# Streaming encoder step: the bias table's product in another PSUM bank and copied by ScalarE, and two more weight units in the second pair of split buffers

## The chip, the core and the metric

The kernel is one program on one core of one Trainium2 chip. The metric is the time that one execution takes on the device, in microseconds (us), as the median of several executions. The engines are TensorE (PE in the profile; PEld is its loading of weights), VectorE (DVE), ScalarE (ACT), GpSimd (POOL) and SyncE (SP, which here only issues DMAs). They run side by side and wait for each other by semaphores.

## What is computed

One inference step of a hybrid encoder layer, for a prompt of 512 tokens and 8 x 16 sample tokens, 640 tokens in all. Cut to what matters here:

```python
h = rms_norm(x, p['norm1_g'])
proj = h @ p['w_in']                                   # 1024 x 4424, all in float32
q, k, v, qi, ki, wi, p_rw, ga, gb = split_cols(proj, IN_SPLITS)
att = dsa_attention(q, qi, wi, k_all, v_all, ki_all, q_pos, k_pos, rel_bias)
rw, wkv_T = rwkv7_mix(p_rw, shift0, wkv0, p)
mixed = sigmoid(ga) * (att @ w_att_out) + sigmoid(gb) * (rw @ w_rw_out)
x = x + mixed @ p['w_out']
x = x + square(relu(rms_norm(x) @ w_ff1)) @ w_ff2
# in dsa_attention:
bias = rel_bias[t5_bucket(sel_pos - qp)]               # 32 buckets x 8 heads, by relative position
```

## The kernel before

**Layout and products.** Activations lie by channel, 128 partitions by 8 groups (`KD`) of 640 tokens (`T`). Each float32 product is made of three products of float32r halves: high by high, low by high, high by low. So every weight and every activation is split into a high and a low part. Weights stream in as units of 128 x 512 (`UNIT`): SP loads unit u into `w_raw` (4 slots), GpSimd's `split` (lines 665 to 676) writes the high part (two instructions, lines 672 and 673) and the low part (line 675), and TensorE multiplies. `w_split` counts units that are split, `w_used` units that TensorE is done with.

**The first tiles.** The input projection has 25 tiles of 128 columns (`WIN_TILES`), two units each. Tiles 0 to 3 are multiplied in pairs by `first_tiles` (lines 805 to 829): tiles 0 and 1 into the two halves of the PSUM tensor `acc`, tiles 2 and 3 into `wk_lo` and `wk_hi`, the halves of the other PSUM tensor `wk`. They run on x times g1, since the norm is not known yet. Their units are 0 to 7, of which four at a time lie split: `w_hi`/`w_lo` and, lower in the scratch area, `w_hi_2`/`w_lo_2`, two slots each. From unit 8 on only `w_hi`/`w_lo` are used, so the split of unit u waits until TensorE has used unit u - 2. Tile n from 4 on is `gemm(2 * n, ...)` and `gemm(2 * n + 1, ...)`, lines 898 to 904. Tile 5 (`TILE_K`, units 10 and 11) holds the keys.

**Around the norm.** ScalarE makes the high parts of x times g1 (`x_high`, line 1477) and the squares (`x_square`, line 1483). VectorE makes the low parts (`x_rest`, line 2011) and adds the squares (`x_add`, line 2019). TensorE's `x_stat` (lines 801 and 802) gives the mean square. VectorE then makes the reciprocal root (`newton`), scales x with it (line 2035), and once more low parts are made, of the normed x (`rest_again`, line 2040). Tile 4 is the first that uses the normed x, and waits for its low parts one group at a time (`each=(h_low, ...)`).

**The bias table.** TensorE multiplies the 32 x 8 bias table with a one-hot matrix, 8 x 768 out (lines 793 and 794), into `acc`, bank half 1, where tile 1 goes. VectorE copies it negated into `line` (line 2006) before all its other work; TensorE waits for that copy (`line_ready`) before tile 1. The table is stored to DRAM from tile 5 on.

**What sets the order.** Each engine's order is written out by hand, one block per engine. GpSimd, VectorE and ScalarE each run their instructions strictly in order.

Of the kernel before, what the change touches and what calls it, by code (L numbers as in the profile page):

```python
# [309 lines left out]
def build(nc, dram):  # L310
# [130 lines left out]
    with ExitStack() as ctx:  # L441
# [220 lines left out]
        def _(pool):  # L662
# [15 lines left out]
            def split_units(lo, hi):  # L678

                u = lo  # L680
                while u < hi and (u % RAW or u < RAW or hi - u < 2 * RAW):
                    split(u, 16 * (u // RAW + 1), u - SPLIT + 1 if u >= SPLIT else None, u + 1)
                    u += 1
                if u < hi:
                    with pool.Fori(u // RAW, hi // RAW) as i:
                        for r in range(RAW):
                            split(r, i * 16 + 16, i * RAW + (r - SPLIT + 1), i * RAW + (r + 1))
                    for u in range(hi // RAW * RAW, hi):
                        split(u, 16 * (u // RAW + 1), u - SPLIT + 1, u + 1)

            for u in range(PAIR):
                split(u, 16 * (u // RAW + 1), u - RAW + 1 if u >= RAW else None, u + 1,
                      *((w_hi_2, w_lo_2) if u % RAW >= SPLIT else (w_hi, w_lo)))
            for u in range(PAIR, PAIR + SPLIT):
                split(u, 16 * (u // RAW + 1), u - RAW + 1, u + 1)
            split_units(PAIR + SPLIT, U_GATE + 2)

            pool.wait_ge(masks_in, 16)
            def norm_y(i):
# [72 lines left out]
        def _(pe):  # L772
            mm, tr = nc.tensor.matmul, nc.tensor.transpose

            def gemm(u, out, first, last, x_hi, x_lo, k0, slot=None, each=None):

                pe.wait_ge(w_split, u + 1)
                s = u % SPLIT if slot is None else slot
                for b in range(4):
                    if each is not None:  # L780
                        sems, base_ = each
                        pe.wait_ge(sems[b % len(sems)], base_ + b // len(sems) + 1)
                    w_h, w_l = w_hi[:, s, b * P:(b + 1) * P], w_lo[:, s, b * P:(b + 1) * P]
                    for n, (w_, x_) in enumerate(((w_h, x_hi), (w_h, x_lo), (w_l, x_hi))):
                        go, end = first and b == 0 and n == 0, last and b == 3 and n == 2
                        mm(out[:, 0:CUT], w_, x_[:, k0 + b, 0:CUT], start=go, stop=end)  # L786
                        done = mm(out[:, CUT:T], w_, x_[:, k0 + b, CUT:T], start=go, stop=end)  # L787
                done.then_inc(w_used, 1)
# [1 line left out]


            pe.wait_ge(table_in, 16 * N_TABLE)
            mm(acc[0:NH, 1, A0:A0 + CUT], rb[:], onehot[:, 0:CUT], start=True, stop=True)
            mm(acc[0:NH, 1, A0 + CUT:A0 + LINE], rb[:], onehot[:, CUT:LINE], start=True, stop=True).then_inc(line_mm, 1)


            def x_stat():
# [6 lines left out]
            def first_tiles(n):  # L804

                outs = (wk_lo, wk_hi) if n else tile_acc
                for k0 in range(0, KD, 2):
                    half = k0 // 4
                    his, los = (w_hi, w_hi_2)[half], (w_lo, w_lo_2)[half]
                    for t in range(2):  # L810
                        if k0 % 4 == 0:
                            pe.wait_ge(w_split, RAW * n + 2 * half + t + 1)
                        if n == 0 and k0 == 0 and t == 1:
                            pe.wait_ge(line_ready, 1)
                        if n and k0 == 0 and t == 0:
                            pe.wait_ge(rms_read, 1)
                        for k in (k0, k0 + 1):
                            if n == 0 and t == 0:
                                pe.wait_ge(h_low[k % 2], k // 2 + 1)
                            b = k % 4  # L820
                            w_h, w_l = his[:, t, b * P:(b + 1) * P], los[:, t, b * P:(b + 1) * P]
                            for m, (w_, x_) in enumerate(((w_h, h_hi), (w_h, h_lo), (w_l, h_hi))):
                                go, end = k == 0 and m == 0, k == KD - 1 and m == 2
                                for cols in COLUMNS:
                                    done = mm(outs[t][:, cols], w_, x_[:, k, cols], start=go, stop=end)  # L825
                        if k0 % 4 == 2:
                            done.then_inc(w_used, 1)
                    if n == 0 and k0 == 4:
                        x_stat()
# [68 lines left out]
            first_tiles(1)  # L898
            for n in range(4, WIN_TILES):
                pe.wait_ge(*freed(n - 2 if n >= 6 else n - 4))  # L900
                gemm(2 * n, tile_acc[n % 2], True, False, h_hi, h_lo, 0, each=(h_low, KD // 2) if n == 4 else None)
                score_units(*SCORE_GAPS.get((n, 0), (0, 0)))
                sample_steps(*SAMPLE_GAPS.get((n, 0), (0, 0)))
                gemm(2 * n + 1, tile_acc[n % 2], False, True, h_hi, h_lo, 4, each=(h_low, KD // 2 + 2) if n == 4 else None)
                if phase(n - 1)[1] == 2 and 1 <= phase(n - 1)[0] <= 4:
                    bonus_sums(phase(n - 1)[0] - 1)
                score_units(*SCORE_GAPS.get((n, 1), (0, 0)))
                sample_steps(*SAMPLE_GAPS.get((n, 1), (0, 0)))
                if n == 4:
                    pe.wait_ge(const_in, 16 * N_CONST)  # L910

                    pe.wait_ge(*freed(2))
                    pe.wait_ge(h_full, KD + 2)
                    for t in range(NT):
                        done = tr(wk[:, 0, t * NH:(t + 1) * NH], wit[HD:HD + NH, t * P:(t + 1) * P], ident[HD:HD + NH, HD:HD + NH])
                    done.then_inc(wi_turned, 1)
                j, step = phase(n)
                if step == 0 and 1 <= j <= 4:
                    key_squares(j - 1)
                if step == 1 and 0 <= j <= 3:  # L920
                    codes(j)
# [544 lines left out]
        def _(act):  # L1466
# [12 lines left out]
            def x_square(k):  # L1479

                if k >= 3:
                    act.wait_ge(sum_set, k - 2)
                do(A((wk_lo, wk_hi)[k % 2][:, 0:T] if k else sq[:, 0, :], xT[:, k, :], ACT.Square), sq_ready)

            act.wait_ge(vec_in, 16)
            for i in range(4):
                act.wait_ge(x_in[i], 16)
                if i < 3:
                    x_high(2 * i)
                    x_high(2 * i + 1)  # L1490
                x_square(2 * i)
                x_square(2 * i + 1)
            x_high(6)
            x_high(7)
            act.wait_ge(sq_used, 1)
# [489 lines left out]
        def _(dve):  # L1985
# [15 lines left out]
                do.settle()  # L2001
                do(V.scalar_tensor_tensor(rs, tmp, 1.5, rs, ALU.add, ALU.mult), signal)


            dve.wait_ge(line_mm, 1)
            do(V.tensor_scalar(line[:], acc[0:NH, 1, A0:A0 + LINE], -1.0, None, ALU.mult), line_ready)

            def x_rest(k):

# [636 lines left out]
```

## Time and profile before

| | us |
|---|---|
| median of 3 executions | 1149.45 |
| lowest and highest | 1149.07, 1151.77 |
| the profiled execution | 1146.9 |
| its span | 1144.9 |
| TensorE busy in it | 1100.8 (96%) |
| VectorE busy | 695.0 (61%) |
| GpSimd busy | 630.1 (55%) |
| ScalarE busy | 398.1 (35%) |

The span runs from the first to the last instruction of the profiled execution; its own time is 2.0 us longer. All places below are in us from the start of the span. In a row of the timeline or of the groups, `L2006` is line 2006 of the kernel, `x2` means that two instructions are merged into one row, and the brackets say how long the engine sat idle before the row and what ended that. A matmul of 384 columns and its partner of 256 columns appear as separate rows or as one row of two.

### The profile page before, as it was taken

The page shows a single profiled execution, that of the slowest core. Times are in us where ns is not written, and L with a number is a line of the kernel's source. Part 1 is how long each engine was busy: PE and PEld are TensorE (multiplying, and loading weights), DVE is VectorE, ACT ScalarE, POOL GpSimd, SP SyncE. Part 2 cuts the span into 40 slices and gives each one's busy share as a digit, 9 for nine tenths or more (in the row PEclk, how much of TensorE's full clock was granted, in tenths as well). Part 3 has the DMA queues.
Part 4 walks back from the last instruction along what each step waited for, and adds up shares of the span by engine and source line. Part 5 has one row for each costly group of instructions (what it writes and reads, how often), then busy time and mean ns, then how long its engine had stood idle before and what let it go on. Part 6 is the DMA issues. An engine that isn't in the chain of part 4 may idle for free.

```text
span 1144.9 us, 25256 instructions
## 1 busy us (share of the span) xinstructions
PE 1100.8 (96%) x10421; PEld 1038.1 (91%) x10421; DVE 695.0 (61%) x1173; ACT 398.1 (35%) x757; POOL 630.1 (55%) x687
## 2 busy tenths in 40 slices
PE   7999999989999999999999999999999999999996
PEld 6878989879888889887899999999999999999995
DVE  6863776773555388765344434676358547745777
ACT  4443334443333343333341122343134223413453
POOL 5742456651322047533236655678568857866783
PEclk9999999999999999999999999999999999999998
DMA  7343533220100232222232223222323133113122
GB/s 248 84 88 66 84 91 88 65 90 4 40 3 3 86 101 61 64 76 74 67 136 74 74 74 102 82 74 74 93 73 92 49 100 91 58 56 110 55 75 92
DMA packets 48342, 89.37 MB, mean 78 GB/s; under 512 B 6728, under 2 KB 11216, under 8 KB 48048
## 3 DMA queue, kind: packets, MB, share of 16 engines
q1 hardware_dynamic: 43568, 77.88, 22.6%
q10 hardware_dynamic: 4672, 10.04, 4.3%
q8 instruction: 76, 1.25, 0.5%
q14 instruction: 26, 0.21, 0.1%
HBM read 80.06 MB, written 7.83 MB: 77 GB/s over the span
## 4 chain that ended last, share of the span: by engine, by line
PE 70%; DVE 20%; issue 4%; ACT 4%; POOL 1%; DMA 0%; ACTq 0%; DVEq 0%; POOLq 0%
PE acc L786 17%; PE acc L787 11%; PE wk L1424 8%; PE acc L1424 7%; PE wk L786 6%; PE wk L787 4%; PE wk L940 2%; PE acc L1020 2%; DVE hid_lo L2435 1%; PE acc L1000 1%; PE acc L1022 1%; DVE invs L2228 1%; PE acc L825 1%; PE wk L1306 1%; DVE xT L2035 1%
## 5 line engine op out<-in xcount | busy, mean ns | idle before, releaser
L675 POOL TENSOR_TENSOR w_lo<-w_raw,w_hi 128x512 fp32r<-128x512 f32 x178 | 243.2, 1366 | 14.8
L672 POOL TENSOR_TENSOR w_hi<-w_raw,ones_w 128x32 fp32r<-128x32 f32 x178 | 60.0, 337 | 323.4 <-PE acc L787 260.8
L786 PE MATMUL acc<-h_hi,w_hi 128*128 128x384 f32 x424 | 150.5, 355 | 6.9 <-POOL w_lo L675 4.3
L786 PE MATMUL acc<-h_lo,w_hi 128*128 128x384 f32 x424 | 143.7, 339 | 0.0
L786 PE MATMUL acc<-h_hi,w_lo 128*128 128x384 f32 x424 | 143.7, 339 | 0.0
L673 POOL TENSOR_SCALAR w_hi<-w_raw 128x480 fp32r<-128x480 f32 x178 | 119.7, 672 | 0.0
L787 PE MATMUL acc<-h_lo,w_hi 128*128 128x256 f32 x424 | 118.7, 280 | 0.0
L787 PE MATMUL acc<-h_hi,w_hi 128*128 128x256 f32 x424 | 118.7, 280 | 0.0
L787 PE MATMUL acc<-h_hi,w_lo 128*128 128x256 f32 x424 | 118.6, 280 | 0.0
L786 PEld LDWEIGHTS acc<-h_hi,w_hi 128*128 128x128 f32 x424 | 79.9, 188 | 15.6 <-issue 9.5
L750 POOL TENSOR_TENSOR p_lo<-w_sum,p_hi 128x512 fp32r<-128x512 f32 x44 | 64.9, 1477 | 29.3 <-ACT p_hi L1942 29.3
L787 PEld LDWEIGHTS acc<-h_hi,w_hi 128*128 128x128 f32 x424 | 80.1, 189 | 0.3
L787 PEld LDWEIGHTS acc<-h_lo,w_hi 128*128 128x128 f32 x424 | 80.0, 189 | 0.0
L787 PEld LDWEIGHTS acc<-h_hi,w_lo 128*128 128x128 f32 x424 | 79.9, 189 | 0.0
L786 PEld LDWEIGHTS acc<-h_hi,w_lo 128*128 128x128 f32 x424 | 79.9, 188 | 0.0
L786 PEld LDWEIGHTS acc<-h_lo,w_hi 128*128 128x128 f32 x424 | 79.9, 188 | 0.0
L1911 ACT ACTIVATE squares<-scaled 128x640 f32<-128x640 f32 x32 | 23.7, 741 | 128.6 <-DVE scaled L2442 128.6
L722 POOL TENSOR_TENSOR merge<-br,e_masks 128x512 f32<-128x512 f32 x19 | 24.8, 1316 | 60.8 <-PE acc L1000 30.7
L2228 DVE TENSOR_TENSOR invs<-invs,acc 128x512 f32<-128x512 f32 (+1 forms) x38 | 25.5, 672 | 47.7 <-PE acc L1022 47.4
L2492 DVE TENSOR_TENSOR x<-x,wk 128x320 f32<-128x320 f32 x64 | 30.1, 483 | 26.6 <-PE wk L1424 26.1
L1424 PE MATMUL wk<-hid_hi,p_hi 128*128 128x320 f32 x144 | 44.8, 311 | 1.4 <-DVE scaled L2442 1.3
L2492 DVE TENSOR_TENSOR x<-x,acc 128x320 f32<-128x320 f32 x64 | 30.1, 482 | 26.1 <-PE acc L1424 25.7
(453 smaller groups left out, 3237.8 us busy)
## 6 DMA issues: line engine op xcount, KB each, us to landing
w_raw<-w SPq DMA_DIRECT2D x178, 256.0 KB, 2.6
w_block<-w SPq DMA_DIRECT2D x64, 256.0 KB, 3.0
line_scratch<-line ACTq DMA_DIRECT2D x8, 384.0 KB
xT<-xT SPq DMA_DIRECT2D x4, 640.0 KB, 6.8
x<-xT ACTq DMA_DIRECT2D x1, 2560.0 KB, 9.8
bias_p<-line_scratch SPq DMA_DIRECT2D x8, 256.0 KB, 4.5
kc<-k_cache SPq DMA_DIRECT2D x8, 256.0 KB, 2.6
vc<-v_cache SPq DMA_DIRECT2D x8, 256.0 KB, 2.7
```

The costliest lines, as they stand in the source:

```text
L672: nc.gpsimd.tensor_tensor(hi[:, s, 0:LEAD], w_raw[:, r, 0:LEAD], ones_w[:], ALU.mult).then_inc(w_high, 1)
L673: nc.gpsimd.tensor_scalar(hi[:, s, LEAD:], w_raw[:, r, LEAD:], 1.0, 1.0, ALU.mult, ALU.mult).then_inc(w_high, 1)
L675: nc.gpsimd.tensor_tensor(lo[:, s, :], w_raw[:, r, :], hi[:, s, :].bitcast(F32), ALU.subtract).then_inc(w_split, 1)
L722: nc.gpsimd.tensor_tensor(merge[n % 2][:], br[i % 2][:, :, 0, :], over_heads(m, NH), ALU.mult).then_inc(merge_set, 1)
L750: nc.gpsimd.tensor_tensor(lo, factor(FACTORS[k % PRODUCTS][0]), hi.bitcast(F32), ALU.subtract).then_inc(p_split, 1)
L786: mm(out[:, 0:CUT], w_, x_[:, k0 + b, 0:CUT], start=go, stop=end)
L787: done = mm(out[:, CUT:T], w_, x_[:, k0 + b, CUT:T], start=go, stop=end)
L940: return mm(out, lhsT, rhs, start=start, stop=True, skip_group_check=True)
L1424: done = mm(out, w_[:, b * P:(b + 1) * P], x_[:, b, x, :], start=first and b == 0 and m == 0, stop=b == PAIRS - 1 and m == 2, skip_group_c ...
L1911: A(squares[:, r, :], scaled[:, r, :], ACT.Square).then_inc(hid_sq, 1)
L2228: do(V.tensor_tensor(dst, dst, src, ALU.add), inv_set)
L2492: V.tensor_tensor(x, x, product_banks(quarter, g)[FACTORS[n][2]], op).then_inc(out_read, 1)
```

## The change

The table's product goes to `wk_lo` in place of `acc`, and TensorE no longer waits for its copy. The copy is taken from VectorE's queue and put in ScalarE's, behind the squares of the first two groups; ScalarE waits there for the product, and for its own copy to end. Units 10 and 11 are split into `w_hi_2`/`w_lo_2`, so their splits wait until TensorE is done with units 6 and 7, the last of tiles 2 and 3, and no longer with units 8 and 9, which are tile 4's. Units 12 and 13 go to `w_hi`/`w_lo` and wait for units 8 and 9. From unit 14 on the rule is the old one.

```diff
-            for u in range(PAIR):
+            for u in range(PAIR + RAW):
                 split(u, 16 * (u // RAW + 1), u - RAW + 1 if u >= RAW else None, u + 1,
                       *((w_hi_2, w_lo_2) if u % RAW >= SPLIT else (w_hi, w_lo)))
-            for u in range(PAIR, PAIR + SPLIT):
+            for u in range(PAIR + RAW, PAIR + RAW + SPLIT):
                 split(u, 16 * (u // RAW + 1), u - RAW + 1, u + 1)
-            split_units(PAIR + SPLIT, U_GATE + 2)
+            split_units(PAIR + RAW + SPLIT, U_GATE + 2)
...
             pe.wait_ge(table_in, 16 * N_TABLE)
-            mm(acc[0:NH, 1, A0:A0 + CUT], rb[:], onehot[:, 0:CUT], start=True, stop=True)
-            mm(acc[0:NH, 1, A0 + CUT:A0 + LINE], rb[:], onehot[:, CUT:LINE], start=True, stop=True).then_inc(line_mm, 1)
+            mm(wk_lo[0:NH, 0:CUT], rb[:], onehot[:, 0:CUT], start=True, stop=True)
+            mm(wk_lo[0:NH, CUT:LINE], rb[:], onehot[:, CUT:LINE], start=True, stop=True).then_inc(line_mm, 1)
...
-                        if n == 0 and k0 == 0 and t == 1:
-                            pe.wait_ge(line_ready, 1)
...
-                gemm(2 * n, tile_acc[n % 2], True, False, h_hi, h_lo, 0, each=(h_low, KD // 2) if n == 4 else None)
+                halves = (w_hi_2, w_lo_2) if n == TILE_K else (w_hi, w_lo)
+                gemm(2 * n, tile_acc[n % 2], True, False, h_hi, h_lo, 0, None, (h_low, KD // 2) if n == 4 else None, *halves)
...
                 x_square(2 * i)
                 x_square(2 * i + 1)
+                if i == 0:
+                    act.wait_ge(line_mm, 1)
+                    do(A(line[:], wk_lo[0:NH, 0:LINE], ACT.Copy, scale=-1.0), line_ready)
+                    do.settle()
...
-            dve.wait_ge(line_mm, 1)
-            do(V.tensor_scalar(line[:], acc[0:NH, 1, A0:A0 + LINE], -1.0, None, ALU.mult), line_ready)
```

ScalarE's queue at the start. `line` is the table, `h_hi` the high parts, `x_in` the landing of x, two groups each. Before:

```order
L1477 ACTIVATE h_hi<-xT,vec 128x640 [waits x_in0,vec_in]
L1477 ACTIVATE h_hi<-xT,vec 128x640
L1483 ACTIVATE sq<-xT 128x640
L1483 ACTIVATE wk<-xT 128x640
L1477 ACTIVATE h_hi<-xT,vec 128x640 [waits x_in1]
```

After:

```order
L1476 ACTIVATE h_hi<-xT,vec 128x640 [waits x_in0,vec_in]
L1476 ACTIVATE h_hi<-xT,vec 128x640
L1482 ACTIVATE sq<-xT 128x640
L1482 ACTIVATE wk<-xT 128x640
L1494 ACTIVATE line<-wk 8x768 [waits line_mm]
L1476 ACTIVATE h_hi<-xT,vec 128x640 [waits x_in1,line_ready]
```

The copy stands ahead of the high part of group 2, which now also waits for it.

GpSimd's queue at units 9 and 10 (three rows a unit). `w_hi_106` and `w_lo_107` are `w_hi_2` and `w_lo_2`. Before:

```order
L672 TENSOR_TENSOR w_hi<-w_raw,ones_w 128x32 [waits w_used,w_landed1]
L673 TENSOR_SCALAR w_hi<-w_raw 128x480
L675 TENSOR_TENSOR w_lo<-w_raw,w_hi 128x512 [waits w_high]
L672 TENSOR_TENSOR w_hi<-w_raw,ones_w 128x32 [waits w_used,w_landed2]
L673 TENSOR_SCALAR w_hi<-w_raw 128x480
L675 TENSOR_TENSOR w_lo<-w_raw,w_hi 128x512 [waits w_high]
```

After:

```order
L672 TENSOR_TENSOR w_hi<-w_raw,ones_w 128x32 [waits w_used,w_landed1]
L673 TENSOR_SCALAR w_hi<-w_raw 128x480
L675 TENSOR_TENSOR w_lo<-w_raw,w_hi 128x512 [waits w_high]
L672 TENSOR_TENSOR w_hi_106<-w_raw,ones_w 128x32 [waits w_used,w_landed2]
L673 TENSOR_SCALAR w_hi_106<-w_raw 128x480
L675 TENSOR_TENSOR w_lo_107<-w_raw,w_hi_106 128x512 [waits w_high]
```

The sequence of instructions is the same; what moved is the buffer of units 10 and 11, and with it the count of `w_used` that they wait for.

## Rows read from the trace of the kernel before

**Rows 1.** Waits, TensorE, 0 to 100 us: total, times, longest (us).

```profile
PE acc L793 <- DMA onehot<-onehot: 6.6, 1, 6.6
PE acc L786 <- POOL w_lo L675: 2.1, 1, 2.1
PE acc L825 <- DVE h_lo L2011: 1.9, 1, 1.9
PE acc L786 <- DVE h_lo L2040: 0.4, 2, 0.2
```

**Rows 2.** Timeline, TensorE at the start: start us, us, instructions.

```profile
6.64 1.44 PE L793 MATMUL acc<-onehot,rb 32*8 32x384 f32 x2 [6.64 <-DMA onehot<-onehot]
...
11.28 0.87 PE L825 MATMUL acc<-h_hi,w_hi 128*128 128x384 f32 x2 [1.92 <-DVE h_lo L2011]
...
13.55 0.73 PE L825 MATMUL acc<-h_lo,w_hi 128*128 128x384 f32 x2
14.09 0.73 PE L825 MATMUL acc<-h_hi,w_lo 128*128 128x384 f32 x2
...
15.15 0.46 PE L825 MATMUL acc<-h_lo,w_hi 128*128 128x384 f32 x2
15.44 0.45 PE L825 MATMUL acc<-h_hi,w_lo 128*128 128x384 f32 x2
...
23.66 0.81 PE L801 MATMUL wk<-sq,const 128*128 128x384 f32 x2
```

**Rows 3.** Timeline, VectorE, 9 to 29 us.

```profile
9.40 0.94 DVE L2006 TENSOR_SCALAR line<-acc 8x768 f32<-8x768 f32 x1 [8.24 <-PE acc L794]
10.28 1.66 DVE L2011 SCALAR_TENSOR_TENSOR h_lo<-xT,vec,h_hi 128x640 fp32r<-128x640 f32 x2
...
21.74 0.82 DVE L2019 TENSOR_TENSOR sq<-sq,wk 128x640 f32<-128x640 f32 x1
```

**Rows 4.** Timeline, ScalarE, 5 to 13 us.

```profile
5.79 1.55 ACT L1477 ACTIVATE h_hi<-xT,vec 128x640 fp32r<-128x640 f32 x2 [2.15 <-DMA xT<-xT]
...
8.50 1.53 ACT L1477 ACTIVATE h_hi<-xT,vec 128x640 fp32r<-128x640 f32 x2
```

**Rows 5.** Timeline, GpSimd, 30 to 53 us.

```profile
30.59 0.83 POOL L672 TENSOR_TENSOR w_hi<-w_raw,ones_w 128x32 fp32r<-128x32 f32 x1
31.40 1.17 POOL L673 TENSOR_SCALAR w_hi<-w_raw 128x480 fp32r<-128x480 f32 x1
32.65 1.74 POOL L675 TENSOR_TENSOR w_lo<-w_raw,w_hi 128x512 fp32r<-128x512 f32 x1
...
40.16 1.73 POOL L675 TENSOR_TENSOR w_lo<-w_raw,w_hi 128x512 fp32r<-128x512 f32 x1
46.63 4.23 POOL L672 TENSOR_TENSOR w_hi<-w_raw,ones_w 128x32 fp32r<-128x32 f32 x1 [4.74 <-PE acc L787]
50.83 0.59 POOL L673 TENSOR_SCALAR w_hi<-w_raw 128x480 fp32r<-128x480 f32 x1
51.50 1.26 POOL L675 TENSOR_TENSOR w_lo<-w_raw,w_hi 128x512 fp32r<-128x512 f32 x1
52.72 0.25 POOL L672 TENSOR_TENSOR w_hi<-w_raw,ones_w 128x32 fp32r<-128x32 f32 x1
```

**Rows 6.** Timeline, VectorE, 28 to 49 us.

```profile
28.40 10.43 DVE L2035 SCALAR_TENSOR_TENSOR xT<-xT,vec,rstd 128x640 f32<-128x640 f32 x8
...
45.71 3.01 DVE L2040 TENSOR_TENSOR h_lo<-xT,h_hi 128x640 fp32r<-128x640 f32 x4
```

**Rows 7.** Timeline, TensorE around the start of tile 5.

```profile
52.91 0.66 PE L786 MATMUL acc<-h_hi,w_hi 128*128 128x384 f32 x1 [2.07 <-POOL w_lo L675]
```

**Rows 8.** By stretch: busy us and count per engine, granted clock (PEclk).

```profile
52.91:56.09 3.18, 3.18 (x12) 3.18 (x13) 0.00 (x0) 0.00 (x0) 1.89 (x3) 0.50 0.90 185
```

**Rows 9.** Timeline around 757 us: VectorE, then GpSimd, both inputs in SBUF.

```profile
757.29 1.58 DVE L2435 TENSOR_TENSOR hid_lo<-hid_sum,hid_hi 128x320 fp32r<-128x320 f32 x1
...
756.98 1.54 POOL L750 TENSOR_TENSOR p_lo<-w_sum,p_hi 128x512 fp32r<-128x512 f32 x1
```

More of the change, by code:

```diff
@@ L773, in _, with gemm @@
             mm, tr = nc.tensor.matmul, nc.tensor.transpose
-            def gemm(u, out, first, last, x_hi, x_lo, k0, slot=None, each=None):
+            def gemm(u, out, first, last, x_hi, x_lo, k0, slot=None, each=None, his=w_hi, los=w_lo):
                 pe.wait_ge(w_split, u + 1)
@@ L782, in gemm @@
                         pe.wait_ge(sems[b % len(sems)], base_ + b // len(sems) + 1)
-                    w_h, w_l = w_hi[:, s, b * P:(b + 1) * P], w_lo[:, s, b * P:(b + 1) * P]
+                    w_h, w_l = his[:, s, b * P:(b + 1) * P], los[:, s, b * P:(b + 1) * P]
                     for n, (w_, x_) in enumerate(((w_h, x_hi), (w_h, x_lo), (w_l, x_hi))):
@@ L900, in _ @@
                 pe.wait_ge(*freed(n - 2 if n >= 6 else n - 4))
-                gemm(2 * n, tile_acc[n % 2], True, False, h_hi, h_lo, 0, each=(h_low, KD // 2) if n == 4 else None)
+                halves = (w_hi_2, w_lo_2) if n == TILE_K else (w_hi, w_lo)
+                gemm(2 * n, tile_acc[n % 2], True, False, h_hi, h_lo, 0, None, (h_low, KD // 2) if n == 4 else None, *halves)
                 score_units(*SCORE_GAPS.get((n, 0), (0, 0)))
                 sample_steps(*SAMPLE_GAPS.get((n, 0), (0, 0)))
-                gemm(2 * n + 1, tile_acc[n % 2], False, True, h_hi, h_lo, 4, each=(h_low, KD // 2 + 2) if n == 4 else None)
+                gemm(2 * n + 1, tile_acc[n % 2], False, True, h_hi, h_lo, 4, None, (h_low, KD // 2 + 2) if n == 4 else None, *halves)
                 if phase(n - 1)[1] == 2 and 1 <= phase(n - 1)[0] <= 4:
```

## Prediction

> **What bounds the kernel now.** The page comes first: TensorE is busy for 1100.8 of 1144.9 us, so a change gains only where it takes idle time or slow running from TensorE, or from what TensorE waits for. The second view is TensorE's list of waits in the first 100 us [rows 1]; the reader is to see two that the change aims at: 1.9 us before the first tile, for VectorE's first low part, and 2.1 us before tile 5, for GpSimd's split of unit 10. The third is the timeline. At the start [rows 2] the table's product runs from 6.64 to about 9.36, then TensorE idles 1.92 us until 11.28, and its pace says that it begins at the lower of its two clock levels: the starts of two successive rows (a row is a pair of matmuls over 640 columns) are 0.54 us apart up to 15.1, and 0.29 after it. VectorE takes the table's copy at 9.40, and only then the low parts [rows 3], although ScalarE had the first high part at about 6.6 [rows 4]. Around tile 5, GpSimd sits idle from 41.9 to 46.6, since unit 8 is in use, and then needs 4.23 us for an instruction of 32 columns [rows 5], while VectorE runs instructions with two inputs in SBUF back to back (0.75 us each in [rows 6], starts and ends touching). TensorE starts tile 5 at 52.91 after 2.07 us of idling [rows 7], and until 56.09 its granted clock is 0.50, which is the 1.2 GHz level [rows 8].
>
> **The start.** Out of VectorE's queue go 0.9 us of copy and the wait for the product. The first low part can then be made from 6.6 on, beside the product, and is there by 7.5. TensorE is released by the end of its own product: 9.4 in place of 11.28, so 1.9 us earlier. What this is worth depends on the clock. Until 15.13 TensorE ran 3.85 us at 0.54 us a row where 0.29 is the faster pace, so a slow microsecond costs 0.46 us. If the clock still rises at 15.13, 1.9 us more run slowly and the gain is 1.9 x 0.54 = 1.0 us. If it rises as long after the first tile's start as it did (3.85 us, so at 13.25), the gain is 1.9 us. If TensorE's work counts from the product on, because the gap between the two is gone, it rises at 6.64 + 3.85 = 10.5, and another (13.25 - 10.5) x 0.46 = 1.3 us come on top: 3.2. No row shows which; before, the idle 1.92 us lay between. I take 2.2, between the second and the third, and keep 1.0 to 3.2.
>
> The Trainium skill (TensorE: Matmul & The Clock Gate, Part 1) states that the point of the rise differs from run to run of one kernel; a single profile cannot show that. It would make each of the three figures a matter of the run, and is one more reason to keep the range.
>
> **The price on ScalarE.** No row has this copy on ScalarE. The nearest above is the high part of 640 columns, 1.55 us for two [rows 4], the nearest below the two squares between 7.34 and 8.50, 0.6 each; with 768 columns that bounds the copy by 0.7 and 0.95. I take 0.85, since a copy is what the high part is. It waits for the product's end at 9.36, so the high part of group 2 moves from 8.50 to about 10.3, and its low part comes at about 12.0. TensorE wants that after four steps (two groups, two tiles) of three rows, 9.4 + 12 x 0.54 = 15.9, or 13.5 with an early rise. Covered, by over a microsecond. The sums of squares came at 22.56 (21.74 + 0.82 [rows 3]) and were wanted at 23.66 [rows 2]. They are now wanted at about 21.5. VectorE ran almost without a gap from 9.40 on; it now begins 2.8 us earlier than with the copy, and stands still for about 1.8 us before group 2, of a total of 0.9 + 2.8: it is ahead by about 1.9, so at 20.7. Hidden, with some 0.8 us to spare; without that cover the price would be up to 1 us of the 2.2.
>
> **Tile 5.** Units 10 and 11 may be split as soon as units 6 and 7 are used, and these end with tiles 2 and 3, before tile 4 begins. So GpSimd goes on from unit 9 at 41.9 (40.16 + 1.73 [rows 5]) with hardly a pause. That removes TensorE's 2.07 us. And without that pause the clock should not fall: 3.18 slow microseconds at 0.46 are 1.46 us. Together 3.5 us.
>
> **What that is paid with.** Unit 10's split now runs beside VectorE's low parts of the normed x, which tile 4 waits for group by group, and which already hold it up by 0.4 us [rows 1]. The two engines hinder each other. Beside VectorE's scaling of x a unit takes 0.83 + 1.17 + 1.74 = 3.74 us [rows 5], against 0.25 + 0.59 + 1.26 = 2.1 alone (the rows from 50.83 on). VectorE's eight instructions take 10.43 us there, 1.30 each, against 0.75 each in the undisturbed run of four in 3.01 [rows 6]. So VectorE loses about 8 x 0.55 = 4.4 us to some 2.8 units, or 1.55 a unit. In the changed kernel units 10, 11 and most of 12 (free once unit 8 is used, in the middle of tile 4) fall on the low parts of groups 1 to 7: about 3 x 1.55 = 4.65 us. The last low part, before at 45.71 + 3.01 = 48.72, comes at 53.4 before the start's gain is taken off. Then TensorE has one group, three rows of 0.29, and the small transposes behind the tile, for which I allow 0.4: tile 5 would start at 54.7 where it started at 52.91, which is 1.8 us lost. From there it runs at the faster pace, 1.46 gained. Net 0.3 lost. So the 3.5 us are real, but a bill of about 3.8 comes with them, and it lies in tile 4. What becomes late next is VectorE's low part of group 4 (line 2040), at the head of unit 9.
>
> Bounds of that bill: nothing, if the waits of one another fall on gaps, and 3 x 1.9 = 5.7 if each unit costs VectorE its whole blocked row and a part of unit 13 comes in too.
>
> **The sum**, against the profiled execution's own 1146.9 (span 1144.9 and 2.0 around it): start -2.2, tile 5 -3.5, tile 4 +3.8, together -1.9 or, rounded, -2: 1144.9. After tile 5 nothing of the change is left, and TensorE's waits for VectorE and GpSimd there are on work that TensorE itself releases, so I take the 2 us to reach the end. The profiled execution lies 2.55 under the median of 1149.45. On the median scale the forecast is 1147.4.
>
> **A rule against this change.** The low parts and the split both have their inputs in SBUF. At 756.98 GpSimd and VectorE take turns: VectorE's instruction from 757.29 lasts 1.58 us and GpSimd's from 756.98 1.54 [rows 9]. But at 46.63 GpSimd did not get its turn for 4.23 us, the rest of VectorE's run, five times as long as one of its instructions [rows 5, 6]. The Trainium skill (SBUF — State Buffer, Who interferes with whom) says that VectorE with two SBUF inputs and GpSimd share a port pair as an exclusive lock, held for a whole instruction, and that the second to issue blocks until the first has finished. By that rule the row of 4.23 should have been under 1; row 46.63 disagrees, rows 9 agree. The rule gives turns, as my sum has it; the row of 4.23 gives the second rival below.
>
> **Rivals.** (a) *Locked out.* As at 46.63, GpSimd gets nothing while VectorE's run lasts. For it: the same engines, the same instruction of VectorE. Against it: there GpSimd came from idling into a run in full flow, now it comes straight from unit 9, having just made VectorE wait, as in the steady turns of 28.4 to 38.8. Then tile 4 is not delayed, unit 10 is ready 2.1 us after the run's end as before, and of tile 5's 3.5 us nothing is gained: -2.2, 1147.2.
>
> (b) *The whole gain.* The turns cost TensorE nothing, because the delayed low parts are not the ones it waits for. Against it: tile 4 waited for them twice already. -2.2 - 3.5 = -5.7, 1143.7.
>
> (c) *Slower.* The delay in tile 4 exceeds what start and tile 5 give back. With a late rise of the clock (-1.0), the upper bound of the bill (+5.7), and a pause before unit 9 of over 2 us, which drops the clock as the 2.07 us did and leaves it low into tile 5, so that of 3.5 only 2.07 come: -1.0 - 2.1 + 5.7 = +2.6, 1152.0. It decides once the bill is above some 5 us, or 1.7 a unit.
>
> (d) *It does not do what it says:* something else holds the first tile, such as unit 0's split or x. Unit 0 was split before 6.6 and x lay there at 5.79 [rows 4]. 2 in 100, time as before.
>
> **How the numbers follow.** Turns with about the bill worked out: 0.46, 1147.4, on its own 1145.9 to 1148.9. (a) 0.21, (b) 0.18, (c) 0.13, (d) 0.02. The forecast is the likeliest, 1147.4. For 8 in 10 the range has to reach near (b) and part of (c), and the runs of before alone spread over 2.7 us: 1143.6 to 1150.6. A difference under 0.3% (3.4 us, 1146.0 to 1152.9) can hardly be told from none. Faster by more than that: (b) and the best part of the turns, with the early rise of the clock, 0.24. Slower by more: only the far end of (c), 0.05. Within: 0.71.
>
> **What would show it.** In the changed kernel's timeline: TensorE's first tile at 9.4, and where its rows go from 0.54 to 0.29 apart (10.5, 13.3 or 15.1); VectorE's last sum of squares before TensorE's line 801. In tile 4: rows of line 2040 at 1.3 us and more in place of 0.75, a wait of TensorE for `h_lo` of 2 us or so before unit 9, and GpSimd's rows of unit 10 at about 0.8, 1.2 and 1.7 right behind unit 9. No wait for GpSimd at tile 5. I am wrong in the mechanism if line 2040 keeps 0.75 us, and in the size if tile 5's first matmul comes under 49 (b) or over 53.5 (c).

## The result, and the profile after

The changed kernel takes 1146.32 us in the median of 22 runs (1140.53 to 1150.39), against 1148.87 for 22 runs of the kernel before beside them (1145.88 to 1152.38). The ratio is 0.9975, with a 95% interval of 0.9964 to 0.9987: 2.5 us by the medians, 2.9 by the ratio. The forecast was 2.05 less than before.

| | before | after |
|---|---|---|
| profiled execution, its span | 1146.9, 1144.9 | 1146.62, 1144.8 |
| product's first matmul / first tile | 6.64 / 11.28 | 6.56 / 9.21 |
| clock rises | 15.13 | 12.58 |
| sum of squares taken (line 801's product) | 23.66 | 21.41 |
| tile 4 / tile 5 / tile 6 begin | 42.72 / 52.91 / 63.91 | 40.47 / 52.04 / 61.61 |

TensorE's waits in the first 100 us (columns as in [rows 1]):

```profile
PE wk L793 <- DMA onehot<-onehot: 6.6, 1, 6.6
PE acc L786 <- DVE h_lo L2040: 2.0, 3, 1.1
```

Both waits of before that the change aims at are gone, the 1.9 for the first low part and the 2.1 for unit 10. The wait for `h_lo`, 0.4 in [rows 1], is 2.0. Now the starts of TensorE, ScalarE and VectorE, from the timeline (three fences in this order), to be laid beside [rows 2 to 4]; the tile's line is 823 here, the high part's 1476, and the copy, line 1494, is ScalarE's:

```profile
7.80 1.48 PE L794 MATMUL wk<-onehot,rb 32*8 32x384 f32 x2
9.21 0.90 PE L823 MATMUL acc<-h_hi,w_hi 128*128 128x384 f32 x2
```

```profile
9.32 0.80 ACT L1494 ACTIVATE line<-wk 8x768 f32<-8x768 f32 x1 [0.92 <-PE wk L794]
10.15 1.55 ACT L1476 ACTIVATE h_hi<-xT,vec 128x640 fp32r<-128x640 f32 x2
```

```profile
6.58 1.68 DVE L2011 SCALAR_TENSOR_TENSOR h_lo<-xT,vec,h_hi 128x640 fp32r<-128x640 f32 x2 [5.42 <-ACT h_hi L1476]
...
11.01 1.68 DVE L2011 SCALAR_TENSOR_TENSOR h_lo<-xT,vec,h_hi 128x640 fp32r<-128x640 f32 x2 [1.76 <-ACT h_hi L1476]
...
16.16 3.58 DVE L2019 TENSOR_TENSOR sq<-sq,wk 128x640 f32<-128x640 f32 x4
```

The low part is made at 6.58, beside the product, and the tile follows the product at once. The copy costs 0.80, its delay of group 2 reaches VectorE (11.01) and stops there: TensorE never waits for it, and the last sum of squares, at 19.7, is 1.7 us ahead of its use at 21.41 (the forecast had 0.8 to spare).

Then tile 4. VectorE, GpSimd and TensorE, against [rows 5 to 7]:

```profile
38.52 5.55 DVE L2040 TENSOR_TENSOR h_lo<-xT,h_hi 128x640 fp32r<-128x640 f32 x4
44.00 0.73 DVE L2045 TENSOR_TENSOR qit<-qit,rstd 128x512 f32<-128x512 f32 x1
44.66 0.86 DVE L2048 TENSOR_TENSOR qis<-qis,rstd 64x128 f32<-64x128 f32 x2
45.45 3.02 DVE L2040 TENSOR_TENSOR h_lo<-xT,h_hi 128x640 fp32r<-128x640 f32 x4
...
50.40 1.27 DVE L2060 TENSOR_SCALAR half_b<-vec 128x8 f32<-128x8 f32 x1
```

```profile
39.61 0.83 POOL L672 TENSOR_TENSOR w_hi<-w_raw,ones_w 128x32 fp32r<-128x32 f32 x1
40.41 1.16 POOL L673 TENSOR_SCALAR w_hi<-w_raw 128x480 fp32r<-128x480 f32 x1
41.65 1.74 POOL L675 TENSOR_TENSOR w_lo<-w_raw,w_hi 128x512 fp32r<-128x512 f32 x1
...
45.27 6.38 POOL L675 TENSOR_TENSOR w_lo<-w_raw,w_hi 128x512 fp32r<-128x512 f32 x1
```

```profile
44.13 0.44 PE L786 MATMUL acc<-h_hi,w_hi 128*128 128x384 f32 x1 [0.69 <-DVE h_lo L2040]
...
46.40 0.41 PE L786 MATMUL acc<-h_hi,w_hi 128*128 128x384 f32 x1 [1.12 <-DVE h_lo L2040]
...
52.04 0.44 PE L786 MATMUL acc<-h_hi,w_hi 128*128 128x384 f32 x1
```

Two things happen one after the other. Up to 45.3 the engines take turns: unit 10's three rows last 0.83, 1.16 and 1.74, and the first four low parts 5.55 instead of 4.00. Of the four, the first lasts 1.80 in both traces, beside unit 9. The other three last 0.81 each in the trace of before, and here, beside unit 10:

```profile
40.25 0.87 DVE L2040 TENSOR_TENSOR h_lo<-xT,h_hi 128x640 fp32r<-128x640 f32 x1
...
41.04 1.20 DVE L2040 TENSOR_TENSOR h_lo<-xT,h_hi 128x640 fp32r<-128x640 f32 x1
...
42.16 1.91 DVE L2040 TENSOR_TENSOR h_lo<-xT,h_hi 128x640 fp32r<-128x640 f32 x1
```

That is 1.55 us for one unit. From 45.3 on, VectorE's second four run undisturbed, in 3.02 as in [rows 6], and GpSimd's one instruction for unit 11 lasts 6.38: it is locked out until VectorE's run of two-input instructions ends near 50.4. No one waits for unit 11 then.

The granted clock, by stretch, columns as in [rows 8]:

```profile
46.70:50.10 3.40, 3.40 (x15) 0.50 0.02 6
394.87:405.11 10.24, 10.09 (x113) 0.50 0.25 77
```

In this profile the clock is at its lower level for 3.4 us inside tile 4, where before it was so inside tile 5. The second stretch is far from the change, with TensorE busy all through it, and accounts for the rest: tile 6 begins 2.30 us earlier, yet the two spans are equal. The same instructions of TensorE ahead of the stretch, behind it, and one tile on, first before, then after:

```profile
396.38 0.68 PE L940 MATMUL wk<-state,ar 64*64 64x64 f32 x16 [1.08 <-DVE state L2236]
...
409.25 0.49 PE L1279 MATMUL acc<-kT,qT 64*128 64x128 f32 x4
...
411.68 0.41 PE L786 MATMUL acc<-h_hi,w_hi 128*128 128x384 f32 x1 [1.72 <-POOL w_lo L675]
```

```profile
393.39 0.68 PE L939 MATMUL wk<-state,ar 64*64 64x64 f32 x16 [1.08 <-DVE state L2236]
...
410.69 0.49 PE L1278 MATMUL acc<-kT,qT 64*128 64x128 f32 x4
...
411.56 0.44 PE L786 MATMUL acc<-h_hi,w_hi 128*128 128x384 f32 x1 [0.15 <-ACT gt L1777]
```

The changed kernel is 2.99 us ahead, then 1.44 behind, then 0.12 ahead. So the stretch takes 4.4 us from TensorE, of which some 1.6 would have been spent waiting for GpSimd anyway, and costs 2.9. The profile of before has no such stretch; four of the thirteen profiles taken for this study have one, near 395 us.

### The profile page after: what moved, and what is told of

Same layout as the page of the kernel before. It is cut to its first block, busy times and chain, and to the rows that moved or that the text cites. A ratio compares the mean times of both kernels' runs of the same rounds, so it can differ in the third digit from the quotient of the medians.

```text
span 1144.8 us, 25249 instructions
## 1 busy us (share of the span) xinstructions
PE 1104.5 (96%) x10421; PEld 1042.0 (91%) x10421; DVE 693.5 (61%) x1172; ACT 398.5 (35%) x758; POOL 634.3 (55%) x687
## 3 DMA queue, kind: packets, MB, share of 16 engines
q1 hardware_dynamic: 43568, 77.88, 22.3%
## 4 chain that ended last, share of the span: by engine, by line
PE 73%; DVE 20%; ACT 4%; issue 2%; POOL 0%; DMA 0%; ACTq 0%; DVEq 0%; POOLq 0%
PE acc L786 17%; PE acc L787 11%; PE wk L1423 8%; PE acc L1423 7%; PE wk L786 6%; PE wk L787 4%; PE wk L939 3%; PE acc L1019 2%; DVE hid_lo L2435 1%; PE acc L1021 1%; PE acc L999 1%; DVE invs L2228 1%; PE acc L823 1%; PE acc L1278 1%; PE wk L1305 1%
## 5 line engine op out<-in xcount | busy, mean ns | idle before, releaser
L675 POOL TENSOR_TENSOR w_lo<-w_raw,w_hi 128x512 fp32r<-128x512 f32 x178 | 247.4, 1390 | 14.8
L1914 ACT ACTIVATE squares<-scaled 128x640 f32<-128x640 f32 x32 | 23.7, 741 | 128.7 <-DVE scaled L2442 128.7
```

The lines of the kernel that those rows point to most:

```text
L675: nc.gpsimd.tensor_tensor(lo[:, s, :], w_raw[:, r, :], hi[:, s, :].bitcast(F32), ALU.subtract).then_inc(w_split, 1)
L1914: A(squares[:, r, :], scaled[:, r, :], ACT.Square).then_inc(hid_sq, 1)
```

## The experiments

Each was run beside the kernel before on the same chip. The questions: does the start carry the whole gain; is the wait in tile 4 made by GpSimd's turns; what holds GpSimd when it is locked out; what does the clock add. All marks are starts of TensorE's matmuls, from the timelines; "4 to 6" is the time from tile 4's first matmul to tile 6's, and "fall" says that a slow stretch of 3.41 us lies in it, which costs about 3.41 x 0.46 = 1.6.

| kernel | first tile | tile 4 | tile 5 | 4 to 6 | fall | ratio to before, 95% |
|---|---|---|---|---|---|---|
| before | 11.28 | 42.72 | 52.91 | 21.2 | yes | |
| the change | 9.21 | 40.47 | 52.04 | 21.1 | yes | 0.9975 [0.9964, 0.9987] |
| e8, the change again | 9.01 | 41.20 | 51.21 | 19.6 | no | 0.9979 [0.9963, 0.9995] |
| e1, start only | 9.15 | 40.10 | 50.30 | 19.7 | no | 0.9984 [0.9965, 1.0002] |
| e2, units only | 11.39 | 43.69 | 53.70 | 19.6 | no | 0.9999 [0.9985, 1.0012] |
| e3, small splits | 8.96 | 40.65 | 48.89 | 17.8 | no | 0.9951 [0.9931, 0.9972] |
| e4, low parts first | 9.11 | 41.16 | 50.28 | 22.3 | yes | 0.9979 [0.9965, 0.9993] |
| e5, start + break | 8.96 | 40.74 | 48.95 | 17.8 | no | 0.9946 [0.9929, 0.9963] |
| e6, change + settle | 9.64 | 41.19 | 53.68 | 22.1 | yes | one run, 1145.39 |
| e7, high by ScalarE | 8.93 | 40.86 | 51.09 | 19.8 | no | 0.9973 [0.9955, 0.9991] |
| e9, change + break | 9.29 | 40.97 | 50.99 | 19.8 | no | 0.9992 [0.9976, 1.0007] |
| e10, break alone | 11.48 | 43.37 | 51.56 | 17.7 | no | 0.9980 [0.9968, 0.9992] |
| e11, e5 again | 8.87 | 41.00 | 49.19 | 17.7 | no | 0.9967 [0.9953, 0.9982] |

### The two halves: e1 and e2

e1 keeps the start of the changed kernel and gives the units back:

```diff
-            for u in range(PAIR + RAW):
+            for u in range(PAIR):
...
-            for u in range(PAIR + RAW, PAIR + RAW + SPLIT):
+            for u in range(PAIR, PAIR + SPLIT):
...
-                halves = (w_hi_2, w_lo_2) if n == TILE_K else (w_hi, w_lo)
+                halves = (w_hi, w_lo)
```

> The start alone: the table's product in the other bank and its copy on ScalarE, units 10 and 11 split as before. Theory A (the gain is the start, and what tile 5 wins is paid in tile 4): the first tile starts at 9.2 to 9.4, tile 5 waits about 2 us for unit 10's split as in the kernel before, the clock falls there again, and the time is 2 to 2.5 us under the kernel before (ratio 0.9978 to 0.9983), the same as the full change within 0.7 us. Theory B (the unit part has a gain of its own, since tile 5 started without a wait): this kernel gains 1.0 to 1.5 us only and is 1 us or more slower than the full change.

e2 keeps the units and gives the start back (the product in `acc`, VectorE's copy, TensorE's wait for it):

```diff
-            mm(wk_lo[0:NH, 0:CUT], rb[:], onehot[:, 0:CUT], start=True, stop=True)
+            mm(acc[0:NH, 1, A0:A0 + CUT], rb[:], onehot[:, 0:CUT], start=True, stop=True)
...
-                    do(A(line[:], wk_lo[0:NH, 0:LINE], ACT.Copy, scale=-1.0), line_ready)
...
+            do(V.tensor_scalar(line[:], acc[0:NH, 1, A0:A0 + LINE], -1.0, None, ALU.mult), line_ready)
```

> The units alone: units 10 and 11 in the second pair of split buffers, the table's product and copy as before. Theory A: no difference to the kernel before, within 0.7 us; TensorE waits 1 to 2 us for line 2040 in tile 4, and not for GpSimd at tile 5. Theory B: 1 to 1.5 us faster.

The start alone has a ratio of 0.9984 (medians 1143.45 and 1145.8), the units alone 0.9999. The interval of the first reaches 1.0002, so its time alone does not prove a gain; the first tile at 9.15 in its trace does. e1's waits and GpSimd's row, then e2's waits:

```profile
PE acc L786 <- POOL w_lo L675: 2.1, 1, 2.1
PE acc L786 <- DVE h_lo L2040: 0.4, 2, 0.2
```

```profile
44.01 4.24 POOL L672 TENSOR_TENSOR w_hi<-w_raw,ones_w 128x32 fp32r<-128x32 f32 x1 [4.74 <-PE acc L787]
```

```profile
PE acc L786 <- DVE h_lo L2041: 2.0, 3, 1.1
PE acc L825 <- DVE h_lo L2012: 1.9, 1, 1.9
```

The unit part exchanges one wait for another of the same size: 2.1 for GpSimd against 2.0 minus 0.4 for VectorE and a tile 4 that is otherwise 0.4 longer. From tile 4 to tile 6 the four kernels need the same 19.6 us, once 1.6 is taken off where the clock fell. e1 also waits 2.1 us before tile 5, as before did, and its clock does not fall:

```profile
50.10:53.50 3.40, 3.20 (x22) 1.00 0.92 188
```

So a pause of that length does not settle whether the clock falls.

### The cause of the wait in tile 4: e3, e4, e7

e3 is the changed kernel with units 10 and 11 split in 64 of their 512 columns only; the rest of these two units' high and low parts is left out.

```diff
+                nc.gpsimd.tensor_scalar(hi[:, s, cols], w_raw[:, r, cols], 1.0, 1.0, ALU.mult, ALU.mult).then_inc(w_high, 1)
...
+                low = slice(0, UNIT) if cols.start == LEAD else cols
+                nc.gpsimd.tensor_tensor(lo[:, s, low], w_raw[:, r, low], hi[:, s, low].bitcast(F32),
...
+                      *((w_hi_2, w_lo_2) if u % RAW >= SPLIT else (w_hi, w_lo)),
+                      cols=slice(480, UNIT) if u in (10, 11) else slice(LEAD, UNIT))
```

> The full change, but GpSimd splits only 64 of 512 columns of units 10 and 11 (three instructions of 32 columns each), so the rest of tile 5's weights are what units 6 and 7 left: that part of the computation is left out. Theory A (GpSimd's splits take turns with VectorE and delay the low parts that tile 4 waits for): tile 4's low parts at line 2040 come at 0.75 us each, no wait of TensorE for them beyond 0.4 us, no fall of the clock, tile 5 starts at about 48, and the time is 3 us or more under the full change. Theory B (tile 4's waits have another cause, such as the high parts on ScalarE): the waits stay and the time is within 1 us of the full change.

The wait for low parts falls to 0.6 us, and tile 5 begins at 48.89, 2.3 us before e8's. VectorE's time from its first four low parts to its second four is 5.13 us (38.71 to 43.84), against 4.94 before (40.77 to 45.71) and 6.93 in the changed kernel (38.52 to 45.45). GpSimd issues as many instructions here as there, so its turns cost by their length, not by their number: 0.2 us against 2.0. Here is its third row of unit 11:

```profile
43.67 5.33 POOL L676 TENSOR_TENSOR w_lo<-w_raw,w_hi 128x32 fp32r<-128x32 f32 x1
```

It writes 32 columns and is locked out as the full one was, 5.33 us.

e4 moves all eight low parts ahead of VectorE's other work there:

```diff
+            for k in range(KD):
+                rest_again(k)
             dve.wait_ge(*freed(0))
             do(V.tensor_tensor(kit[:], kit[:], rstd[:], ALU.mult), h_full)
...
-            for k in range(4):
-                rest_again(k)
             query_scaled(1)
-            for k in range(4, KD):
-                rest_again(k)
```

> The full change, and VectorE makes all eight low parts of the normed x (line 2040) before it scales the indexer's key, head weights and first query (lines 2051, 2052, 2045, 2048), which stood before and among them. If the order of VectorE's queue is what makes the turns with GpSimd costly (theory A), the low parts end some 3 us earlier, TensorE's wait for them in tile 4 falls from 2.0 us to under 0.7, and the time falls by 1.5 to 3 us against the full change. If the low parts are bound by their inputs (the high parts from ScalarE, which come at 33 to 43 us) or TensorE then waits for the head weights instead (its transposes at the end of tile 4), it falls by under 0.7 us.

```profile
PE wk L841 <- DVE qis L2048: 2.0, 1, 2.0
PE wk L914 <- DVE wit L2054: 1.5, 1, 1.5
```

```profile
37.58 9.49 DVE L2040 TENSOR_TENSOR h_lo<-xT,h_hi 128x640 fp32r<-128x640 f32 x8
```

The wait for low parts is gone, and what was pushed back is waited for instead, 3.5 us. The eight low parts last 1.2 us on average (0.87, 1.20 and 1.91 in turn), so here the turns went on to the end; GpSimd was never locked out, although VectorE's run has no gap in it. This order does not pay the bill, because the key, the head weights and the query that it pushes back are wanted too.

e7 lets ScalarE write the high parts of units 10 and 11, and leaves GpSimd the two low parts:

```diff
-            act.wait_ge(w_used, 8)
+            for u in (10, 11):
+                act.wait_ge(w_landed[u % RAW], 16 * (u // RAW + 1))
+                act.wait_ge(w_used, u - 3)
+                A(w_hi_2[:, u % SPLIT, :], w_raw[:, u % RAW, :], ACT.Copy).then_inc(ready, 1)
```

> The full change, and ScalarE, not GpSimd, writes the high parts of units 10 and 11 (one copy of 512 columns each, before its high parts of groups 4 to 7), so that GpSimd has one instruction a unit there in place of three. Theory A (the price in tile 4 is one turn per GpSimd instruction): TensorE's wait for line 2040 falls from 2.0 to about 1.0 us and the time by 0.5 to 1.5 us against the full change. If the wait is bound by the high parts of groups 4 to 7, which ScalarE now makes later, it does not fall.

```profile
38.91 6.20 DVE L2050 TENSOR_TENSOR h_lo<-xT,h_hi 128x640 fp32r<-128x640 f32 x4
```

```profile
40.00 3.70 POOL L698 TENSOR_TENSOR w_lo<-w_raw,w_hi 128x512 fp32r<-128x512 f32 x2
...
46.62 4.59 POOL L674 TENSOR_TENSOR w_hi<-w_raw,ones_w 128x32 fp32r<-128x32 f32 x1 [2.92 <-PE acc L794]
```

Two instructions of GpSimd put VectorE's first four back by 2.2 us, about what one and a half whole units did in the change. The wait for `h_lo` is 2.1 as in the change, and the stage 19.8. Less work on GpSimd did not help: this time none of it fell into the lock-out. The 4.59 us are unit 12's, locked out when it came from idling, as in [rows 5].

### What locks GpSimd out, and the better kernel: e6, e5, e10, e11, e9

e6 is the change with a single wait of VectorE for its own last result, in front of the second four low parts:

```diff
             query_scaled(1)
+            do.settle()
             for k in range(4, KD):
                 rest_again(k)
```

> The full change, and VectorE waits for its own last instruction before the low part of group 4, a gap of some 0.1 us in its run. Theory A (an unbroken run keeps GpSimd out): the low part of unit 11 (line 675, 6.4 us in the full change) takes 1.3 to 1.8 us, the turns go on through groups 4 to 7, their low parts take 1.2 us and more each, and TensorE's wait for line 2040 in tile 4 grows from 2.0 to 3.5 us or more; tile 5 starts at 53 or later where it started at 52.0. Theory B (the gap changes nothing): the row stays over 5 us.

```profile
45.99 1.38 POOL L675 TENSOR_TENSOR w_lo<-w_raw,w_hi 128x512 fp32r<-128x512 f32 x1
```

```profile
46.28 5.51 DVE L2040 TENSOR_TENSOR h_lo<-xT,h_hi 128x640 fp32r<-128x640 f32 x4
```

The instruction that lasted 6.36 to 6.38 us in the two profiles of the change lasts 1.38, and the turns go on through the second four, which take 5.51 instead of 3.02. TensorE's wait for low parts grows from 2.0 to 3.1 us, less than the 3.5 expected, and tile 5 moves to 53.68. This is the prediction's picture of turns all through: e6's stage is 20.5 without the clock's fall, against 19.6. A single run's time settles nothing at this size; the rows do.

e5 takes e1 (units as before) and puts seven small instructions, none with two inputs in SBUF, ahead of the scaling of queries 2 and 3:

```diff
-            query_scaled(2)
-            query_scaled(3)
             do(V.tensor_scalar(half_b[:], vec[:, VEC["w0"][0]:VEC["w0"][0] + 8], 0.5, None, ALU.mult))
...
             do(V.memset(amask[0:HD, HD:P], -NEG))
+            query_scaled(2)
+            query_scaled(3)
```

> The start alone (as in e1_start_only), and VectorE's seven small instructions with one input or none (three tensor_scalar, four memsets, lines 2060 to 2066) stand right behind the last low part of the normed x, ahead of the scaling of queries 2 and 3. Theory A (GpSimd was kept out by an unbroken run of VectorE instructions with two inputs in SBUF, and gets in at the first with one): line 672 for unit 10 ends at about 46.4 in place of 48.2 (places of e1_start_only), tile 5's wait falls from 2.1 us to under 0.7, and the time is 1.5 to 3 us under e1_start_only's, ratio to the kernel before about 0.996 to 0.9975. Theory B (that long row has another cause): line 672 still lasts until the end of the scaling, now later, and the kernel is not faster than e1_start_only.

```profile
44.66 2.21 POOL L672 TENSOR_TENSOR w_hi<-w_raw,ones_w 128x32 fp32r<-128x32 f32 x1 [4.75 <-PE acc L787]
46.85 0.58 POOL L673 TENSOR_SCALAR w_hi<-w_raw 128x480 fp32r<-128x480 f32 x1
```

```profile
43.73 3.01 DVE L2040 TENSOR_TENSOR h_lo<-xT,h_hi 128x640 fp32r<-128x640 f32 x4
46.67 0.23 DVE L2058 TENSOR_SCALAR half_b<-vec 128x8 f32<-128x8 f32 x1
```

GpSimd's small instruction ends at 46.87, right where the last low part does (46.74), and no longer at the end of the queries. Its 4.24 us in e1 have become 2.21, TensorE's wait for unit 10 is gone, tile 5 begins at 48.95, and the low parts last as long as before (4.01 and 3.01). Medians: 1142.59 against 1148.43.

e10 is the kernel before with this order alone, and e9 the full change with it, both by the same diff as e5's last one; e11 is e5 without any edit, beside them.

> The kernel before with e5's order of VectorE's small instructions and nothing else. Theory A (the row of 4.2 us before unit 10 is VectorE's unbroken run, and cost TensorE 2.1 us of waiting and often the clock): tile 5's wait falls from 2.1 to about 0.2 us, the start is as before, ratio to the kernel before 0.997 to 0.9985. Theory B: the gain of e5 needs the earlier start as well, and this one gains under 0.8 us.

> The full change together with e5's order (VectorE's seven small instructions right behind the last low part). Theory A (the unit part costs TensorE about 2 us of waits for low parts in tile 4, whatever comes later): tile 4's waits for line 2040 stay at 2 us, tile 5 starts at 51 to 52, and the time is that of the full change within 0.7 us, so 2 us or more over e5. Theory B (with the break the second pair of buffers is worth something on its own): as fast as e5 or faster.

> e5_break_after_lows once more, unaltered, to compare the other two with on the same chip. Theory A: ratio to the kernel before 0.9935 to 0.9965, and the gains add up: its gain is that of the start alone (2 to 2.9 us) and that of e10 together.

e10 has the stage of e5 with the start of before, at a ratio of 0.9980. e11 comes to 0.9967; its stage is e5's to 0.1 us, so the difference from e5's 0.9946 (their intervals overlap) says how far one such comparison can be trusted. Its gain of 0.33% is near that of the start (0.16%, e1) and of the order (0.20%, e10) together. e9 gains nothing in the stage over e8: GpSimd comes out of the lock at 50.12 instead of 52.35, but nobody waits for it, and the wait for the low parts stays at 2.0. Its ratio, 0.9992, is a little worse than e8's, intervals overlapping, at an equal stage; its profile has the slow stretch near 395, e8's has not. The two remedies for tile 5 do not add, and the change of order is the cheaper one.

e8 is the changed kernel without any edit, to have it beside e5 on one chip:

> The full change once more, unaltered, on the same chip as the three others, to compare them with, and for a second profile: by theory A of the clock (its rise depends on chance as well as on the start) the rise comes between 11.9 and 15.2, tile 0 starts at 9.0 to 9.4, and tile 4's waits for line 2040 are again about 2 us. Ratio to the kernel before 0.9965 to 0.9985.

Medians 1145.89 against 1148.43. The same rows as in the first profile of the change:

```profile
39.25 5.55 DVE L2040 TENSOR_TENSOR h_lo<-xT,h_hi 128x640 fp32r<-128x640 f32 x4
```

```profile
45.99 6.36 POOL L675 TENSOR_TENSOR w_lo<-w_raw,w_hi 128x512 fp32r<-128x512 f32 x1
```

The turns and the lock-out come back with their times, 0.01 to 0.02 us apart. The clock's fall in tile 4 does not.

## Why the prediction was right, and where it was not

**The total.** 2.05 us forecast, 2.5 to 2.9 measured, and the likeliest case, turns, is the one that came nearest. Two of its terms were wrong, in opposite directions: one gave about 1.5 us too much, the other took about 1.8 too much. That they nearly cancel is luck.

**The start: right.** -2.2 was taken. From the product to the first tile, TensorE needs 2.65 us instead of 4.64: 2.0 earlier. By the sum of squares at line 801, the ten profiles with the new start come at 21.8 on average (21.0 to 22.5), the three with the old one at 24.2 (23.7 to 24.6). Of these 2.4 us, 0.3 is the table's landing, which varies (product at 6.5 and 6.7 on average), so 2.1 is the change's. This is the middle one of the prediction's three figures, 1.9, and a little. It also says how the clock went: the rise comes 4.5 us after the first tile on average with the product directly ahead of it, and 4.8 without, so the product did not count for it, and the third figure falls. One profile could not have told: in single ones the rise comes 2.7 (e1) to 6.0 us (e4) after the first tile. The Trainium skill (TensorE: Matmul & The Clock Gate, Part 1) has this point differ by half a microsecond either way from run to run. That it differs, the traces confirm; the size they do not: two profiles of one kernel, the change and e8, have 3.4 and 5.5 us.

**ScalarE's price: right.** Bounds of 0.7 to 0.95, 0.85 taken, 0.80 measured; group 2's high part at 10.15 (10.3 forecast), the sum of squares ahead of its use.

**Tile 5, the wait: right, the clock: not.** The 2.07 us went. The 1.46 us for the slow stretch was taken as a sure consequence of the pause. It is not: e1 has the pause and no fall, the change has a fall in its first profile, inside tile 4 after waits of 0.69 and 1.12 us, and none in its second (e8). Of the six profiles in which TensorE waits 2 us or more for low parts in tile 4 (the change twice, e2, e6, e7, e9) two have a fall there. The term was a property of one profile and should have stood in the range alone. By these profiles, this failed step took off about 1.5 us too much.

**Tile 4, the turns: right mechanism, too large.** The forecast had a wait for `h_lo` of about 2 us in tile 4 (2.0), rows of line 2040 at about 1.3 us (0.87, 1.20 and 1.91, 1.33 on average) and unit 10's rows at 0.8, 1.2 and 1.7 (0.83, 1.16, 1.74). What failed was the count: three units at 1.55, 4.65 us on VectorE. Measured are 2.0 (6.93 minus 4.94, below e3): 1.55 from unit 10, exactly the price worked out for a unit, and the rest from the high part of unit 11; then the turns stopped. The bill of 3.8 us on TensorE compares with 2.0: tile 4's first matmul to its small transposes takes 9.61 in e8 and 7.65 in e1. Of these 1.96, 1.6 are in the list of waits. Most of the other 0.36 lies at the same places: counted from start to start against the steady pace, e8's two stops (listed as 0.69 and 1.12) cost 0.95 and 1.35, and e1's one (0.19) costs 0.42. This failed step put on about 1.8 us too much. With turns all through (e6), tile 4's start to tile 5's is 12.49, or 10.9 without the fall, against 10.0 in e8: a bill of about 2.9, so even then the forecast's 3.8 was high.

**Rival (a)** was given 0.21 as a whole case. It came true for the second half of tile 4: one instruction of GpSimd stood for 6.38 us. The reason given against it, that GpSimd comes straight from its last unit as in the steady turns, held for unit 10 and failed for unit 11. The prediction treated turns and lock-out as two cases, where one stage had both. **Rival (b)** is excluded by e3: without the turns' length the stage is 1.8 us shorter than e8's, so the turns did cost TensorE something. **Rival (c)** fell with its bill of 5.7; even e6, with turns to the end, pays about 0.9 more than the change in the stage. **Rival (d)** fell with the first tile at 9.21.

**The size test.** Tile 5's start was to lie between 49 and 53.5, and lies at 52.04, and at 51.21 in e8. The test was too wide to show the error in the bill: the forecast's own sum gives 54.7 - 2.2 = 52.5, and the first profile comes near it only with the clock's fall in it. From tile 4's start to tile 5's the sum has 54.7 - 42.7 = 12.0 us, and e8, without a fall, needs 10.0.

**The lock.** The prediction weighed a rule of the Trainium skill (SBUF — State Buffer, Who interferes with whom): the shared port pair is an exclusive lock held for an instruction, and the one that issues first makes the other block. The turns agree with it (1.74 us for GpSimd's instruction beside VectorE's at 1.39). The 4.24, 5.33 and 6.38 us do not: several of VectorE's instructions went by in them. What the experiments show is what ends such a wait: a pause of VectorE for its own result (e6, 6.37 to 1.38), or an instruction without two inputs in SBUF (e5, 4.24 to 2.21; e9, 6.38 to 4.35). Once GpSimd is kept out, it is the rest of the unbroken run, not one instruction, that it waits for. But a run without a gap does not by itself keep it out: beside e4's eight low parts the turns went on. What decides at the moment of GpSimd's request whether it enters the turns or is kept out, stays open. It was not the length of its instruction (e3), nor whether it came from idling: unit 11 of the change did not and was held, unit 10 of before did and was held, and at 871.61 in the trace of before one that had idled 1.45 us was let in at once (1.59 us, with VectorE's instruction beside it at 1.58).

## What to carry to other kernels

Before another engine's work is moved beside an engine that is waited for, ask whether it can instead be let in at the place where it stands: here seven small instructions in another order on VectorE took away the same 2 us before tile 5 as a second pair of buffers, without the bill. When GpSimd has an instruction far longer than its size in the profile, look at VectorE for a back-to-back run of instructions with two inputs in SBUF, and break the run at the first point where nobody waits for it. And a stretch of low clock in one profile is a term for the range, not for the sum, until a second profile shows it.

## What the runs showed of the chip

- One instruction of GpSimd over 32 columns was held for 4.24 us (e1) and 5.33 us (e3), one over 512 for 6.38, each until VectorE's run of two-input instructions ended or soon after; beside a broken run the same instructions took 2.21 and 1.38.
- In the turns GpSimd's instructions cost VectorE by their length: 1.55 us for a unit in the change (its instructions of 0.83, 1.16 and 1.74 us lengthen VectorE's from 0.81 to 0.87, 1.20 and 1.91), 2.2 for two low parts of 512 columns (e7), 0.2 for the five instructions before the lock-out in e3, with 32 columns each, against 2.0 for the five in the change.
- VectorE in its turn waits when GpSimd is let in: its first instruction behind the run, over 8 columns, lasts 1.27 us in the change and 0.23 in e5, where GpSimd had only 32 columns pending.
- The clock rose 2.7 to 6.0 us after the first tile in thirteen profiles of nearly equal starts. After pauses of about 2 us it fell for 3.41 us in some profiles (before) and not in others (e1).
- Slow stretches of 10.24 us near 395 us, with TensorE busy throughout, lie in the profiles of the change, e4, e7 and e9, and in none of the other nine. In each of the four TensorE loses 4.4 us against the trace of before and gets part of it back from a wait for GpSimd, so 2.9 us are left, as much as the change is worth. What sets them off is open. 21 of the 34 listed runs of the change have a mean granted clock below 0.992, against 32 of the 85 runs of the kernel before beside the experiments; whether the change makes such stretches likelier was not tested.
- Stretches of 3.41 us at the lower clock also lie elsewhere: between 245 and 250 us in seven of the thirteen profiles (e3, e5, e7 to e11), near 90 us in e2, e6 and e8. So spans of single profiles cannot be compared to within 1.6 us.
